# Lane steps of the second block's products moved to even points of the product stream

## What is computed

```python
# layer 1: causal attention with forget gates; layer 2: attention in a window of 128 tokens, RoPE, sinks
# both: x = x + (y * silu(gate)) @ w_out, and an RMS norm after the second
# layer 3 ("second block"):
proj = einsum('btd,dc->btc', h, w_in)
rw = token_shift(proj[..., :RWKV_COLS]); hg = proj[..., RWKV_COLS:]
o_rwkv = rwkv7_branch(rw)    # 16 heads of 64: S = S*w + (S a) b^T + v k^T, o = S r, group norm, * silu(z)
o_hgrn = hgrn2_branch(hg)    # 8 heads of 128: gated linear attention in chunks, RMS norm, * silu(z)
h = layer_norm(ALPHA * h + concat(o_rwkv, o_hgrn) @ w_out)
```

## Time and profile before

| | |
|---|---|
| median of 3 runs | 3457.03 us (3456.93 to 3457.41) |
| the profiled execution | 3456.05 us |
| its span, first to last instruction | 3454.3 us |
| mean granted TensorE clock | 0.984 |
| PE busy | 3267.8 us (95%) |
| DVE busy | 1731.7 us (50%) |
| ACT busy | 1227.9 us (36%) |
| second block's lanes begin | 1937.84 us |
| `out` blocks begin | 3216.23 us |
| the first of them takes | 77.62 us |

### The profile page before, as it was taken

One profiled execution on the slowest core, in us unless ns is written; L12 is line 12 of the kernel. 1 busy time (PEld: TensorE's weight loads), 2 busy tenths in 40 slices (PEclk: granted clock), 3 DMA queues, 4 the chain that ended last, 5 costly groups with the idle time before them and its releaser, 6 DMA issues.

```text
span 3454.3 us, 41106 instructions
## 1 busy us (share of the span) xinstructions
PE 3267.8 (95%) x16498; PEld 2624.6 (76%) x16498; DVE 1731.7 (50%) x2867; ACT 1227.9 (36%) x2166; POOL 71.2 (2%) x132
## 2 busy tenths in 40 slices
PE   7999999999999999999999899998999898989896
PEld 5777777777768887777788687777877787878685
DVE  5444444444433336555633545555555556565544
ACT  4323232323232324333433335343434343434421
POOL 0000000000000000000000000000000000000200
PEclk9999999999999999999999999999999999999998
DMA  4222222222223322222143211111212121111532
GB/s 160 74 74 73 74 74 74 74 74 74 74 83 134 106 80 68 68 68 73 66 171 118 71 56 62 43 62 44 71 46 68 45 66 49 62 55 55 189 128 85
DMA packets 79915, 275.38 MB, mean 80 GB/s; under 512 B 9952, under 2 KB 10592, under 8 KB 78832
## 3 DMA queue, kind: packets, MB, share of 16 engines
q1 hardware_dynamic: 63936, 232.13, 20.0%
q0 software_dynamic: 15792, 40.64, 3.4%
HBM read 252.74 MB, written 19.92 MB: 79 GB/s over the span
## 4 chain that ended last, share of the span: by engine, by line
PE 82%; DVE 11%; ACT 3%; issue 3%; DMA 0%; DVEq 0%; SPq 0%; POOL 0%; ACTq 0%
PE bank L251 13%; PE bank L253 13%; PE bank L252 13%; PE bank L255 7%; PE bank L257 7%; PE bank L256 7%; PE bank L1135 2%; PE bank L1142 2%; PE bank L302 2%; PE bank L275 2%; PE bank L424 1%; PE bank L1203 1%; DVE mc L1076 1%; PE bank L1149 1%; PE bank L451 1%
## 5 line engine op out<-in xcount | busy, mean ns | idle before, releaser
L251 PE MATMUL bank<-ma_split,mc_split 128*128 128x512 f32 x2304 | 981.0, 426 | 38.8 <-DVE ma_split L800 19.1
L253 PE MATMUL bank<-ma_split,mc_split 128*128 128x512 f32 x2304 | 909.6, 395 | 0.0
L252 PE MATMUL bank<-ma_split,mc_split 128*128 128x512 f32 x2304 | 905.5, 393 | 0.0
L665 DVE TENSOR_TENSOR mc_split<-mc,mc_split 128x1024 fp32r<-128x1024 f32 x426 | 519.7, 1222 | 433.7 <-ACT mc_split L514 429.1
L514 ACT ACTIVATE mc_split<-mc 128x1024 fp32r<-128x1024 f32 x426 | 448.4, 1054 | 298.0 <-PE bank L255 256.1
L251 PEld LDWEIGHTS bank<-ma_split,mc_split 128*128 128x128 f32 x2304 | 437.6, 190 | 132.8 <-issue 36.5
L253 PEld LDWEIGHTS bank<-ma_split,mc_split 128*128 128x128 f32 x2304 | 435.8, 189 | 97.3
L252 PEld LDWEIGHTS bank<-ma_split,mc_split 128*128 128x128 f32 x2304 | 438.9, 190 | 74.5 <-issue 6.5
L523 ACT ACTIVATE mc<-bank,stat 128x128 f32<-128x128 f32 (+3 forms) x128 | 67.6, 528 | 553.2 <-DVE stat L673 552.9
L1317 ACT ACTIVATE mc<-bank 128x512 f32<-128x512 f32 x192 | 114.6, 597 | 384.0 <-PE bank L1149 263.9
L255 PE MATMUL bank<-mc_split,ma_split 128*128 128x512 f32 x576 | 230.7, 401 | 5.1 <-DMA ma_split<-y 4.9
(11 more groups left out here) (355 smaller groups left out, 4167.7 us busy)
## 6 DMA issues: line engine op xcount, KB each, us to landing
mc<-in_w SPq DMA_DIRECT2D x426, 512.0 KB, 3.3
x<-mc POOLq DMA_DIRECT2D x8, 1024.0 KB, 5.0
y<-mb_split POOLq DMA_DIRECT2D x28, 256.0 KB, 2.9
ma_split<-y POOLq DMA_DIRECT2D x28, 256.0 KB, 7.2
mb<-in_xt SPq DMA_DIRECT2D x8, 512.0 KB, 15.5
mc<-in_x POOLq DMA_DIRECT2D x4, 1024.0 KB, 9.8
mc<-x POOLq DMA_DIRECT2D x4, 1024.0 KB, 5.9
mb<-x POOLq DMA_DIRECT2D x4, 1024.0 KB, 9.2
```

The costliest lines, as they stand in the source:

```text
L251: mm = pe.matmul(banks[j][:], wh[:, c], act_hi[:, kt, :], start=(kt == 0), stop=False)
L252: pe.matmul(banks[j][:], wl[:, c], act_hi[:, kt, :], start=False, stop=False)
L253: last = pe.matmul(banks[j][:], wh[:, c], act_lo[:, kt, :], start=False, stop=(kt == KT - 1))
L665: dve.tensor_tensor(w_low[:, s % NR, :, :], w_raw[:, s % NR, :, :], w_high[:, s % NH, :, :].bitcast(F32), ALU.subtract).then_inc(w_lo, 1)
```

## The change

The places of three groups of steps change, and nothing else; each engine still runs the same instructions.

```diff
             def rw_at(u, k):
 
                 if k < 5:
-                    return (128 * u - 54 if u else 2) + 3 * k
+                    return (128 * u - 54 if u else 2) + 2 * (3 * k // 2)
                 if k < 9:
                     return 120 * u + 18 + 2 * (k - 5)
                 if k < 59:
                     return 120 * u + 28 + 2 * (k - 9)
-                return 120 * u + 128 + 3 * (k - 59)
+                return 120 * u + 128 + 4 * (k - 59)
 
             def hg_at(h, m):
 
                 rate = {UNITS - 2: 23, UNITS - 1: 20}.get(h, 45)
-                return 64 * (BLOCK_OF["hg", h] + 1 - LANE0) + 1 + m * rate // 10
+                return 64 * (BLOCK_OF["hg", h] + 1 - LANE0) + 2 + 2 * (m * rate // 20)
```

## The result

The changed kernel takes 3500.30 us (median of 4 runs, 3494.72 to 3501.98) against 3456.98 us for the kernel before (4 runs, 3453.86 to 3457.41): ratio 1.0123 (95% interval 1.0109 to 1.0136), so slower by 1.2%. The sign and the mechanism were forecast; the time lies 2 us above the range and 17 above the number.

The account below looks back on a forecast made before the run. PE, busy 95% of the span, was taken to bound the kernel. Terms -6 - 0.5 - 4.5 + 22 + 2.5 + 7 + 6 = +26.5 on 3456.05, plus 1.0 for the median, gave 3483 us, range 3463 to 3498.

Parts of the forecast that it names:

- Clock, +6: PE after new waits of about 3 us: six falls to half clock at 1.0 us, +6 us (bounds 0 and +13).
- third rival: Whole kernel: later G products, clock drops for whole stretches, hg 7 late by 10; about 3495 us, chance 0.18.
- Epilogue, -4.5: Unit ends: k=62 later saves waits but meets rw(u+1, 6) in bank 7, -4.5 us (bounds -9 and +3).
- Everything else, 0: Stalls in all places outside the groups named in the forecast: no difference, 0 us.
- Reciprocal, -0.5: DVE's reciprocal ahead of hg(h, 18): units 2, 5, 6 gain, 3, 4, 7 lose, -0.5 us (bounds -6 and +6).
- Main term, +22: rw(u, 63) in front of rw(u+1, 8): pads and G product come later, +22 us (bounds 4 and 31).
- Rival 1: Hidden pads, at k=63: DVE is early or pads have room, main term only 4; 3458.5 us, chance 0.12.
- Bank 7, -6: rw(u, 1) and hg(h, 17) parted by two points, their conflict covered in 6 units, -6 us (bounds -8 and -4).
- hg 6, +2.5: hg 6's m=2 on ACT behind the X copy and ahead of WR copies, +2.5 us (bounds 0 and +5).
- `out`, +7: First `out` block: hg 7's m=0, m=2, m=3 later, first level product 6.1 late, +7 us (bounds 0 and +10).
- Work on PE, 0: PE instructions: the same, 63 fewer visits save no switches between products and side work, 0 us.

Follow-up runs that it names:

- three copies: Kernel before with ACT's copy L1310 made three times at 120u+144, in front of the pads, k=63's DVE work left at +140: 3473.10 us, ratio 1.0051.
- experiment 4: Kernel before with rw(u, 60..64) at 132, 136, 140, 143 and 148, so k=63 one point earlier than in the change: 3459.48 us, ratio 1.0011.
- experiment 1: Kernel before with k=63 moved to 120u+144 and k=64 to +148: 3483.88 us; changed kernel with k=63 one point later: 3463.62 us.
- one copy: Kernel before with ACT's copy L1310 made once at 120u+144, k=63's DVE work left at +140: 3457.95 us, ratio 1.0004.
- prologue -5.6: Kernel before with only the prologue's offsets changed to 0, 2, 6, 8, 12: 3450.31 us, ratio 0.9980.
- hg +11.6: Kernel before with only the hg steps moved to even places, in all units: 3467.56 us, ratio 1.0033.
- k=63 alone: Kernel before with rw(u, 63) moved to 120u+144 and rw(u, 64) to 120u+148, nothing else: 3483.88 us, ratio 1.0081.
- five copies: Kernel before with ACT's copy L1310 made five times at 120u+144, k=63's DVE work left at +140: 3488.77 us, ratio 1.0097.

## Why the prediction was wrong

By its own steps, in the order of their share in the miss (the change came to +42.8 us against +26.5; no single step makes up the 16.3):

- **Clock, +6: mis-sized; the step that failed first.** Idle time and clock can be told apart in the seven heads. Idle they are 3.26, 3.86, 3.5, 3.28, 1.93, 3.34 and 4.9 us, together 24.1, less the 1.4 us of seven times 0.2 before: 22.7 us, against the forecast 22. The head row of the table has 34.1. The other 11.4 us come with the clock: it fell in six of them, for 3.21 us in unit 4 and 5.71 in unit 1, where I had six falls at 1.0 us for everything.

  The reason given for 1.0, that part of the stretch lies in the wait, is what failed. In unit 4 the stretch covers the products behind the wait in full (2620.84 to 2624.05, all at 0.50). In unit 1 a part does lie in the wait (2122.47 to 2123.59), but the stretch is twice as long, and 5.71 us of it are left behind the wait. The prediction's own row of a stretch at half clock (1.6 us) would have been the right price for the shorter ones, as the three copies then showed, and for the longer ones nothing had been set aside. Six falls in the seven heads is the number forecast, though the forecast had them among nine waits. From the first lane step to the end of the `out` blocks the time at half clock grew by 20.5 us (75.1 to 95.6), worth 10.3 at the most, so part of what the heads lose to the clock other places get back.

  The Trainium skill (TensorE: Matmul & The Clock Gate, Why this matters for your kernels), which the prediction held to be the third rival's rule, warns of idle gaps between bursts of products; that agrees with the six falls behind 3.3 to 4.9 us. Idle times of 1.9 us went both ways: units 2 and 5 of the three copies fell, units 1, 4 and 6 of the same kernel and the head with 1.93 us didn't.
- **Epilogue, -4.5: wrong sign.** +0.9 in the change; in experiment 4 the whole kernel was +2.8 us. (The six values listed add up to -4.7.) The first head was put at 0 and came to +2.6, for the two table loads ahead of L1303; the last, not listed, to +1.7. Of the gains only unit 5's (-2.4, came as -2.2) and the second head's (-1, came as -2.2) were real.
- **Everything else, 0: +4.3 us.** Small, spread over many places, and not followed further.
- **Reciprocal, -0.5: too small, -3.7.** The sign by unit was right for all six, but the gains of 2, 5 and 6 were 2.8, 2.2 and 3.1 us instead of 1.2, 2.0 and 1.4. In unit 2 it is the same mis-sized clock with the other sign. PE's timeline of the changed kernel there, to be held against the last row:

```profile
2222.93 0.66 PE L1149 MATMUL bank<-ident,mc 128*128 128x128 f32 x4 [0.95 <-DVE mc L1076]
```

  The wait is shorter by 1.15 us, as forecast (1.2), and behind it the transposes take 0.66 us instead of 0.91: the fall has gone with it. The windows of the 2.5 us from the start of these transposes, before and then in the change:

```profile
2218.50:2221.00 2.50, 2.50 (x12) 2.40 (x13) 2.08 (x4) 1.12 (x2) 0.00 (x0) 0.55 0.00 0
2222.90:2225.40 2.50, 2.47 (x16) 2.26 (x17) 2.10 (x4) 1.41 (x4) 0.00 (x0) 1.00 0.04 7
```

  Units 5 and 6 were not followed to their rows.
- **Main term, +22: right** in place, mechanism and size (22.7 us idle), by experiment 1 from both sides, and its lower bound too (one copy: 0.6 us a head). By unit it is less exact: unit 5's 1.93 us are made up for by unit 2's 3.86 and unit 3's 3.5. Rival 1 is refuted by the same.
- **Bank 7, -6 (-4.7), hg 6, +2.5 (+3.5), `out`, +7 (+7.2): right,** `out` with some luck in the size. There the chain is the one forecast, each step 1.2 to 1.5 us sooner. Timelines of DVE and PE, where the block begins 35.6 us later than before:

```profile
3272.78 0.69 DVE L1598 SCALAR_TENSOR_TENSOR mb<-mb 128x512 f32<-128x512 f32 x1
...
3285.32 2.05 PE L1203 MATMUL bank<-mb 128*128 128x128 f32 x8 [13.79 <-DVE mb L1581]
```

  m=3 ends at 3273.5 - 35.6 = 3237.9 in the time of before (forecast 3239.1), the first level product starts at 3249.7 (forecast 3251.2, before 3245.07). So it is 4.7 us late where 6.1 were forecast, and what follows it adds 2.5 where 0.9 were; the sum came right by errors that cancel. That the drain of 1.38 us, which the Trainium skill (ScalarE: Activation LUTs, What ACT_TABLE_LOAD costs) adds to a load, is not to be counted here was right as well: in the rows of experiment 4 the exp begins 1.30 us after its load, and the log's load at once behind it.
- **Work on PE, 0: right within 7.1 us of busy time;** the 20.5 us more at half clock are enough for that, though it wasn't told apart.

The third rival, 'more', at 3495 and with a chance of 0.18, is what came by its time: it gave 45 us at the most, and 42.8 came. Of its mechanisms the clock that drops for a whole stretch is the one found; the G product at 31 us and hg 7 late by 10 are not. The range left the top of this rival out, and there the time lay.

**What stays open.** The parts don't add up to the whole: k=63 +28.0, prologue -5.6, hg +11.6, epilogue +2.8 make 36.8 us, the change has 43.3 by the medians. A gap of about that size lies in the epilogue's places: with k=63 alone they cost 24.8 us, 6.1 less than before, perhaps because L1516 and L1517 have left them, and in the change nothing of this remains (31.8). Neither was tried by itself.

## What to carry to other kernels

When a step is moved in engines that work in order, list for each engine what it now stands *ahead of* and *behind*, not only when it comes: a copy that waits for another engine made PE wait some 3 us in front of the work that PE needed next and hardly at all one point behind it, and the evacuation of k=62, moved three points later, came to stand behind two table loads. A wait of some 3 us on PE is to be priced with the half clock that may follow it, here 1.7 to 3.2 us more in six of seven heads. And a common rule for all units (even places) leaves time that a choice by unit finds: the best version moved one step in all units and the reciprocal in three of eight.

## What was not expected of the hardware

- The same idle time did and didn't lower TensorE's clock: with 1.9 us in front of the G product it kept 2.4 GHz in unit 1 of the three copies and fell to 1.2 in unit 2, with 2.4 to 3.2 us (five copies) one head of six kept it, one with 3.21 us.
- The clock stayed at half behind the wait for at least 3.21 us in one head of the change and for 5.71 us in another, behind idle times of 3.28 and 3.26 us; what decided between them the runs don't show. Such longer stretches came in units 1 and 2, those of about 3.2 us in units 3, 4, 6 and 7.
- Time at half clock, added up from the first lane step on, grew with the longer waits: 75.1 us before, 81.9 with three copies, 95.6 with five copies and in the change, 105.8 with k=63 alone, though that kernel is 16 us faster than the change. With one copy it was 64.9, less than before, so differences of 10 us between single executions also come without longer waits.
